# Groups of six expert tiles, sums in two staggered halves and a ring of eight operand tiles in the second product of a PEER layer

## What is computed

```python
def peer_ffn(h, w_query, sub_keys, expert_u, expert_v):
    ...                                        # per token: 8 heads choose 16 experts each (idx, gate)
    def block(args):
        xk, ik, gk = args
        act = jax.nn.gelu(jnp.einsum('tkd,td->tk', expert_u[ik], xk))
        return jnp.einsum('tk,tkd->td', gk * act, expert_v[ik])
    ...
x = x + peer_ffn(rmsnorm(x, norm2), peer_wq, peer_keys, peer_u, peer_v)
y = rmsnorm(x, final_norm)
```

## Time and profile before

| | us |
|---|---|
| median of 3 runs (lowest, highest) | 3221.39 (3219.71, 3221.70) |
| the profiled execution, its own time | 3221.37 |
| its span | 3219.6 |
| last stage (`peer_down`), from its first matmul to the end of the span | 2152.6 to 3219.6 |
| PE busy, of the span | 3107.1 (97%) |
| DVE busy, of the span | 2569.2 (80%) |

### The profile page before, as it was taken

One profiled execution on the slowest core, in us unless ns is written; L12 is line 12 of the kernel. 1 busy time (PEld: TensorE's weight loads), 2 busy tenths in 40 slices (PEclk: granted clock), 3 DMA queues, 4 the chain that ended last, 5 costly groups with the idle time before them and its releaser, 6 DMA issues. The chain is left out here.

```text
span 3219.6 us, 45871 instructions
## 1 busy us (share of the span) xinstructions
PE 3107.1 (97%) x17420; PEld 2726.2 (85%) x17420; DVE 2569.2 (80%) x5687; ACT 883.4 (27%) x1307; POOL 1126.0 (35%) x758
## 2 busy tenths in 40 slices
PE   8999989899999999999999999998999999999998
PEld 7867765499999999999999999987777777777776
DVE  6621244357799999989888988858999999999996
ACT  4210300132122222224444444422222222222222
POOL 0000000000032222223333333324555886688881
PEclk9999989999999999999999999999999999999999
DMA  3010021351187777768888889899999999999993
GB/s 103 15 41 29 14 88 51 99 163 55 49 264 246 246 243 245 243 209 287 294 286 325 288 292 325 285 331 339 343 344 343 336 347 350 339 344 346 347 347 138
DMA packets 359908, 754.88 MB, mean 234 GB/s; under 512 B 37085, under 2 KB 205881, under 8 KB 354041
## 3 DMA queue, kind: packets, MB, share of 16 engines
q0 software_dynamic: 102576, 373.47, 34.3%
q1 hardware_dynamic: 257112, 378.49, 34.0%
HBM read 647.21 MB, written 102.25 MB: 233 GB/s over the span
## 5 line engine op out<-in xcount | busy, mean ns | idle before, releaser
L1931 POOL DMA_INDIRECT lead<-in_peer_v_dram,chosen x212 | 424.2, 2001 | 179.1 <-DVE acc_s L1950 128.1
L1931 POOL DMA_INDIRECT gr_row<-in_peer_u_dram,chosen x205 | 229.8, 1121 | 462.0 <-DVE chosen L1940 454.5
L1907 ACT ACTIVATE up_a<-up_pa 128x352 f32<-128x352 f32 x256 | 118.9, 464 | 755.3 <-PE up_pa L1892 662.5
L1931 POOL DMA_INDIRECT dr_row<-in_peer_v_dram,chosen x140 | 282.6, 2019 | 99.9 <-DVE acc_s L1950 72.4
L2694 DVE TENSOR_TENSOR acc<-pd_po,acc 128x512 f32<-128x512 f32 x384 | 278.7, 726 | 25.5 <-PE pd_po L2761 22.6
L1931 POOL DMA_INDIRECT s_sb<-in_peer_u_dram,chosen x147 | 159.3, 1084 | 374.7 <-DVE chosen L1940 369.1
L1950 DVE SCALAR_TENSOR_TENSOR acc_s<-lead,chosen,acc_s 128x1024 f32<-128x1024 f32 x212 | 279.9, 1320 | 0.0
L2340 ACT ACTIVATE lo_wx<-room 128x704 fp32r<-128x704 f32 x128 | 101.6, 794 | 623.6 <-DVE room L2331 623.6
L1940 DVE CUSTOM_DVE_ANT_0 gr_row<-gr_row,xs 128x1024 f32<-128x1024 f32 x205 | 248.6, 1220 | 14.4 <-DMA gr_row<-in_peer_u_dram,chosen 14.4
L511 PE MATMUL fr_a<-pj_w,h_t 128*128 128x256 f32 (+1 forms) x864 | 199.3, 393 | 0.9 <-PEq L186 0.9
L2462 DVE TENSOR_SCALAR pg_hot_i<-pg_iota,sel_t 128x128 f32<-128x128 f32 x704 | 195.7, 358 | 0.0
(11 more groups left out here) (484 smaller groups left out, 7420.1 us busy)
## 6 DMA issues: line engine op xcount, KB each, us to landing
lead<-in_peer_u_dram SPq DMA_DIRECT2D x128, 512.0 KB
room<-in_peer_v_dram SPq DMA_DIRECT2D x128, 512.0 KB
act_d<-up_a SPq DMA_DIRECT2D x256, 176.0 KB
room<-w_d SPq DMA_DIRECT2D x64, 704.0 KB, 6.6
room<-act_d SPq DMA_DIRECT2D x64, 704.0 KB
w_d<-pg_wb SPq DMA_DIRECT2D x24, 1024.0 KB, 7.0
w_d<-room SPq DMA_DIRECT2D x20, 1024.0 KB
lead<-in_peer_wq_dram SPq DMA_DIRECT2D x20, 512.0 KB, 3.9
```

Of the source, the lines that this page charges most:

```text
L1907: self.nc.scalar.activation(self.a_sb[c][:], self.pa[c][:, 0:WB], ACT.Gelu_apprx_tanh).then_inc(self.a_act, 1)
L1931: pool.indirect_dma_start(self.buf[i % self.n], None, self.table, bass.IndirectOffsetOnAxis(ap=self.idx[:, col:col + 1], axis=0)).then_inc ...
```

## The change

Five things change, all in the last stage. Line numbers shift by 1 above `peer_down` and by about 30 to 45 in it.

- **Groups of six.** `GE` is 6 and the groups are 20 of six tiles and two of four, 22 in place of 32. DVE's additions of a bank go from 384 to 264.
- **Halves and pairs.** A group's twelve outs are summed in two halves of six banks. In a half, three pairs of outs follow each other one tile apart: in step s, pair 0 takes tile s, pair 1 tile s-1, pair 2 tile s-2. PE waits for the operands of one tile at a time. All eight banks are used in turn: the two of `up.pa` join (before, they served only for the small products).
- **One ring.** The operands of eight tiles (the same memory) are a ring; tile m uses slot m mod 8. PE frees tile e of a group once the last pair of the second half has used it (`freed`); ACT waits for that.
- **The order on DVE** follows ticks (one tile in one half, half a tile's matmuls). Before tick 0 it has made 13 steps (of three a tile); then `STEPS_AT` gives the steps of each tick of a group, `ROOM_AT` the share of gathered rows, and additions stand in ticks 0, 4, 5, 6, 10 and 11, two in each. Rows run from tick 6 to tick 248.
- **Start and end.** SP's loads of tiles 2 to 5 come ahead of more of the loads of `acc`. The order of the norm's slots is 6, 7, 0, 1, 8, 2, 5, 3, 4, and the steps of the end are written out.

```diff
-GE = 4
+GE = 6
+RING = 8
...
-        self.nc.scalar.activation(self.vx[m // GE % 2][m % GE][0], self.v[m % 2], ACT.Copy).then_inc(self.v_hi, 1)
+        self.nc.scalar.activation(self.vx[m % RING][0], self.v[m % 2], ACT.Copy).then_inc(self.v_hi, 1)
...
+SIZES = (GE,) * (NK // GE - 1) + (4, 4)
+NG = len(SIZES)
+PLACES = [(g, half, e) for g in range(NG) for half in range(1 if g == NG - 1 else 2) for e in range(SIZES[g])]
+TICKS = len(PLACES) - SIZES[-1]
+AHEAD = 13
+STEPS_AT = (2, 2, 2, 2, 1, 1, 1, 1, 1, 1, 2, 2)
+ROOM_AT = (3, 8, 8, 8, 7, 7, 7, 12, 12, 12, 3, 3)
+ROWS_FROM, ROWS_TO = 6, TICKS
...
             load(2)
+            load(3)
             load_acc(ND - 1)
-            load(3)
+            up.keep(sp, NK - 1, 1)
+            load(4)
             load_acc(0)
-            up.keep(sp, NK - 1, 1)
+            load(5)
             load_acc(1)
-            load(4)
-            load_acc(2)
-            load(5)
-            load_acc(3)
-            load_acc(4)
             up.all_kept(sp)
             load(6)
             load(7)
+            load_acc(2)
+            load_acc(3)
+            load_acc(4)
...
-                if e == 0 and g >= 2:
-                    act.wait_ge(o_done, OUTS * (g - 1))
+                if m >= RING:
+                    g, e = (m - RING) // GE, (m - RING) % GE
+                    if e < GE - 1:
+                        act.wait_ge(freed, (GE - 1) * g + e + 1)
+                    else:
+                        act.wait_ge(filled, sum_at(g, OUTS - 1) + 1)
...
+            for tick, (g, half, e) in enumerate(PLACES):
+                make(made_by(tick), made_by(tick + 1))
+                for i in range(rows_by(tick), rows_by(tick + 1)):
+                    if i == 0:
+                        dve.wait_ge(accs_in, 16 * NXS)
+                    rows_v.add(dve, i, gate, acc_s)
+                if e == 0 and tick >= 1:
+                    for o in (HALF_OUTS - 2, HALF_OUTS - 1):
+                        add(g if half else g - 1, o + (0 if half else HALF_OUTS))
+                if e >= SIZES[g] - 2:
+                    for o in (2 * (e - SIZES[g] + 2), 2 * (e - SIZES[g] + 2) + 1):
+                        add(g, HALF_OUTS * half + o)
...
+            def half_sums(g, half):
+                for step in range(SIZES[g] + HALF_OUTS // 2 - 1):
+                    for pair in range(HALF_OUTS // 2):
+                        e = step - pair
+                        if e < 0 or e >= SIZES[g]:
+                            continue
+                        if half == 0 and pair == 0:
+                            pe.wait_ge(v_lo, FIRST_OF[g] + e + 1)
+                            pe.wait_ge(w_lo, FIRST_OF[g] + e + 1)
+                        for o in range(HALF_OUTS * half + 2 * pair, HALF_OUTS * half + 2 * pair + 2):
+                            if e == 0:
+                                bank_free(sum_at(g, o))
+                            mm = product(g, o, e)
+                            if e == SIZES[g] - 1:
+                                mm.then_inc(filled, 1)
+                    if half == 1 and step >= HALF_OUTS // 2 - 1 and step < SIZES[g] + HALF_OUTS // 2 - 2:
+                        mm.then_inc(freed, 1)
```

More of the change, by code:

```diff
@@ L2612, in _ @@
                 sp.dma_start(acc_s[0:n, NSP + i, :], x2_tiles[NT - 1][first:first + n]).then_inc(accs_in, 16)
-            for m in range(2 * GE, NK):
+            for m in range(8, NK):
                 load(m)
@@ L2708, in weigh, with take, make @@
                                                op0=ALU.mult, op1=ALU.mult).then_inc(ready, 1)
-            def take_samples():
+            def take(at, out):
                 for half in range(2):
-                    dve.wait_ge(folded, half + 1)
-                    nc.vector.tensor_copy(x_s[:, half * W4:(half + 1) * W4], pf[half][0:LAST, :]).then_inc(taken, 1)
-                dve.wait_ge(gain_loaded, 16)
-            def take_half():
-                for half in range(2):
-                    dve.wait_ge(folded, 3 + half)
-                    nc.vector.tensor_copy(acc[0:HALF_P, ND - 1, half * W4:(half + 1) * W4], pf[half][0:HALF_P, :]).then_inc(taken, 1)
-            for m in range(1, GE):
-                lower.multiply(dve, m)
-                lower.low_v(dve, m)
-                lower.low_w(dve, m)
+                    dve.wait_ge(filled, at + half + 1)
+                    nc.vector.tensor_copy(out[:, half * W4:(half + 1) * W4], banks[(at + half) % NBANKS][0:out.shape[0], :]
+                                          ).then_inc(emptied, 1)
+            def make(first, last):
+                for i in range(first, last):
+                    (lower.multiply, lower.low_v, lower.low_w)[i % 3](dve, i // 3)
+            make(3, made_by(0))
             dve.wait_ge(active, 1)
@@ L2751, in _ @@
-            weigh(NT - 2)
-            inverse(NT - 1)
-            weigh(NT - 1)
+            for tick, (g, half, e) in enumerate(PLACES):
[10 more added lines that the diff above has]
+                        add(g, HALF_OUTS * half + o)
@@ new lines, in _ @@
+            g = NG - 1
+            inverse(0)
+            add(g, HALF_OUTS - 2)
+            inverse(1)
+            add(g, HALF_OUTS - 1)
+            take(FOLD_REST, x_s)
+            dve.wait_ge(gain_loaded, 16)
+            weigh(0)
+            inverse(2)
+            weigh(1)
+            add(g, HALF_OUTS)
+            inverse(3)
+            weigh(2)
+            add(g, HALF_OUTS + 1)
+            inverse(4)
+            weigh(3)
+            take(FOLD_HALF, acc[0:HALF_P, ND - 1, :])
+            inverse(5)
@@ L2755, in _ @@
+            weigh(4)
+            add(g, HALF_OUTS + 2)
+            inverse(6)
+            weigh(5)
+            add(g, HALF_OUTS + 3)
+            inverse(7)
+            weigh(6)
+            add(g, HALF_OUTS + 4)
+            weigh(7)
+            add(g, HALF_OUTS + 5)
+            inverse(8)
+            weigh(8)
         @block.tensor
@@ L2760, in product @@
                 for x, y in parts:
-                    mm = nc.tensor.matmul(po[(OUTS * g + o) % NPO][:], lower.tokens(wx[g % 2][e], s, y),
-                                          vx[g % 2][e][x][:, half * W4:(half + 1) * W4],
-                                          start=(e == 0 and (x, y) == parts[0]), stop=(e == GE - 1 and (x, y) == parts[-1]))
-                return mm
-            for e in range(GE):
-                pe.wait_ge(v_lo, e + 1)
-                pe.wait_ge(w_lo, e + 1)
-                for o in range(NPO):
-                    mm = product(0, o, e)
-                    if e == GE - 1:
-                        mm.then_inc(o_done, 1)
@@ new lines, in product, with bank_free @@
+                    mm = nc.tensor.matmul(banks[sum_at(g, o) % NBANKS][:], lower.tokens(wx[m % RING], s, y),
+                                          vx[m % RING][x][:, half * W4:(half + 1) * W4],
+                                          start=(e == 0 and (x, y) == parts[0]), stop=(e == SIZES[g] - 1 and (x, y) == parts[-1]))
+                return mm
+            def bank_free(at):
+                if at == NBANKS - 2:
+                    pe.wait_ge(up.a_act, 2 * NK)
+                if at >= NBANKS:
+                    pe.wait_ge(emptied, at - NBANKS + 1)
@@ new lines, in _ @@
+            for g in range(NG - 1):
+                for half in range(2):
+                    half_sums(g, half)
+            half_sums(NG - 1, 0)
+            pe.wait_ge(shaped, PACKED)
+            pe.wait_ge(rows_v.used, COLS)
+            fold_into(FOLD_REST, LAST, [(fold[i], acc_s[:, NSP + i, :]) for i in range(len(PACKS))])
+            for o in range(HALF_OUTS, OUTS):
+                if sum_at(NG - 1, o) == FOLD_HALF + 2:
+                    pe.wait_ge(emptied, BASE + 2)
+                    fold_into(FOLD_HALF, HALF_P, [(fold[0][:, 0:HALF_P], acc[:, ND - 1, :])])
+                bank_free(sum_at(NG - 1, o))
+                for e in range(SIZES[-1]):
+                    mm = product(NG - 1, o, e)
+                mm.then_inc(filled, 1)
```

126 lines of the change are left out of this document (47 added, 79 removed).

## The result

| | before | after |
|---|---|---|
| median, us (lowest, highest) | 3221.39 (3219.71, 3221.70) | 3187.62 (3185.35, 3191.35) |
| ratio to before, 95% interval | | 0.9897 (0.9880 to 0.9914) |
| profiled execution / its span | 3221.37 / 3219.6 | 3191.35 / 3189.6 |

The change makes the kernel 1.0% faster, 34 us. The forecast was 3176 in a range of 3164 to 3206: the sign is right and the time lies in the range, but it misses the likeliest case's own range (3164 to 3186) by 2 us. That small miss hides a large one, which is the subject of what follows: the forecast said that PE becomes the bound, and it does not. That the number fits is in part luck: errors of opposite sign stand behind it.

A forecast was written before the change was run, and what follows sets the result against it. DVE was taken to bound mid-stage, PE after the change. Last matmul 2152.6 + 995.2 + 5.3 + 10 (start) + 4 (late transfers) = 3167.1; + 6.9 (end) + 1.8 = 3175.8, so 3176 us, range 3164 to 3206.

The forecast's parts named there:

- likeliest case: Whole kernel: the forecast proper, DVE relieved and PE the bound, 3176 us within 3164 to 3186, chance 0.62.
- PE becomes the bound: Mid-stage of `peer_down`: DVE falls to 44.8 us a group of six against PE's 46.65, so 45.1 us of gaps go.
- slack: DVE's spare time per group of six in `peer_down`: 46.65 - 44.8 = 1.8 us, taken to absorb a ring-slot wait.

The follow-up runs named there:

- experiment 6: Changed kernel with each tick's gathered rows placed evenly among its operand steps and additions, none moved to another tick: 3166.80 us, ratio 0.9828 to before.

## What to carry to other kernels

Price an instruction by its distance to the next in the order that it will have: steps that each wait for the one before cost more side by side than between others (1.38 us against 1.19 here). That took 1.2 us a group of a slack that the forecast put at 1.8 and that was 1.4. Read a bound off the number of instructions in a long window, not off busy shares, which here called PE 98.6% busy while DVE set the pace. Where one engine serves two clients, spread the steps that wait for transfers; here an edit to the order alone (experiment 6) was worth some two thirds as much as the whole change.
